# One decoder step with 32 routed experts: the second expert's first gate/up chunks moved ahead of the first one's down products, and the down bias moved into the first combine

## The chip, the cores and the metric
One of the eight cores of a Trainium2 chip runs the kernel, in float32 throughout. The metric is the device time of one execution in microseconds. Before the change it is 1125.2, the median of three runs (1124.46 to 1127.17).

## The reference
288 tokens (256 of a prompt, 8 x 4 of running sequences) of width 1024 go through one layer: windowed attention with sinks beside an S5 state-space branch, an output projection, and then the part that the change is about, a mixture of 32 experts with the top 4 for each token:

```python
logits = x2d @ w_router + b_router
top_v, top_i = lax.top_k(logits, 4)
gates = softmax(top_v)
# for the tokens of each expert e:
h = xb @ w_gate_up[e] + b_gate_up[e]                      # 1024 -> 2048
out = _clamped_swiglu(h) @ w_down[e] + b_down[e]          # 1024 -> 1024
y = segment_sum(out * row_w, row_tok)                     # gate-weighted sum per token
x = x + y
```

The weights of an expert are 8.4 MB (gate/up) and 4.2 MB (down), so all 32 are 403 MB.

## The kernel before, in words
**The layer ahead of the experts** takes the first 190 us and is not touched.

**The order of the experts.** On the device the experts are sorted by how many tokens they have. Experts 0 and 1 come first whatever their number. A place in the order has a fixed kind (KINDS, line 50): "mid" takes 64 slots of tokens, "few" 32, "many" 64 and 32. The first places are mid, mid, few, many, few, mid, few, many. Places 2 to 17 are a loop of four places with four rounds; later places follow in another loop. p is the place, w counts the wide (64-slot) passes so far and s the slim (32-slot) ones. Items that overflow their slots would run in a loop at the end, which has none to do with these inputs.

**The work of one place on TensorE** (expert, line 1052) is written out by hand:
- gate_up, eight chunks of 128 input rows. A wide pass has four matmul calls for a chunk, alternating between two 64-column halves of the array. Each call of float32 is two matmul records in the trace, so a chunk is 8 records. PSUM banks 0 and 1 collect gate and up (bank 5 for slim).
- Between chunks 1 and 2, the gate matrix of the place before is transposed (turn_gates, line 994). Between chunks 3 and 4, and again later, comes one half of combine (line 1008): it multiplies the expert output ye of the place before with the transposed gates gT, and VectorE adds the result to the residual xT (accumulate, line 1974). Half a combine of a wide pass has four calls, two on the upper and two on the lower 64 rows of the array.
- turn_hidden (line 916) transposes gate and up results, which ScalarE and VectorE copy out and turn into hT (hidden, line 1928).
- gather and turn_gathered (lines 855, 873) pick the tokens of the next place with a one-hot matmul into bank 5, and transpose them. ScalarE copies the result to xe, the input of the next gate_up.
- down (line 950): eight chunks of the down product into bank 4, which ScalarE copies to ye.

Place 0 has no place before it. There gate_bias (line 1037) stands in for combine: it adds the gate-weighted down bias of all experts, with bdnT (bias) and gT, four calls for a half, each on another 32 rows. Its four results go through accumulate as well, so that the semaphores comb_done and acc_done count 4 for each place.

**The weights** come through rings in SBUF: gu_ring has four slots of two chunks (2048 KB each), so one expert, and dn_ring four of half a down matrix, so two experts. SyncE's queue issues every load, in a fixed order (load_others, line 370). A load waits for gu_used (one count for each chunk) or dn_used (one for each quarter of a down product), so for TensorE to be done with what lies in the slot. Expert 0's gate/up and both first down matrices are loaded ahead. Expert 1's gate/up follows as eight pieces of 1024 KB, each as soon as the chunk of expert 0 in its place is used (lines 388 to 390). From then on it is, for each place, the down halves of the place two ahead and then the four gate/up slots of the next one but one.

Of the kernel before, what the change touches and what calls it, by code (L numbers as in the profile page):

```python
# [23 lines left out]
P = 128  # L24
# [53 lines left out]
def build(nc, a):  # L78
# [152 lines left out]
    pos_next = sb("pos_next", [3], o); o += 32  # L231
    assert o <= WK + 3456, (o, WK + 3456)
# [12 lines left out]
    bdnT = sb("bdnT", [2 * P], o); o += 1024  # L245
    grid = sb("grid", [ITEM_PART, REPEATS * NE], o); o += sz(ITEM_PART, REPEATS * NE)
# [123 lines left out]
    def load_others(sp):  # L370

        regs = [sp.alloc_register(f"sp_at{k}") for k in range(2)]

        def expert_at(k, p):
            sp.reg_load(regs[k], ord_e[0:1, p:p + 1] if isinstance(p, int) else ord_e[0:1, bass.ds(p, 1)])
            return sp.snap(regs[k], min_val=0, max_val=NE - 1)

        def gu(x, p_before):
            for k in range(GU_SLOTS):
# [73 lines left out]
    def _(sp):  # L453
# [70 lines left out]
        for k, c in enumerate((0, 2, 1, 3)):  # L524
            sp.wait_ge(S("acc_done"), items * 4 + (4 * NE + (4 if k else 2)))
# [7 lines left out]
    def _(pe):  # L533
# [353 lines left out]
        def gate_up(p, w, s, kind, chunks):  # L887
# [6 lines left out]
            for k in chunks:  # L894
# [3 lines left out]
                if kind != "few":  # L898
                    for part in range(2):
                        for h in range(2):  # L900
                            f = part * D + h * HALF
                            last = mm(pb[part][SLOTS * h:SLOTS * h + SLOTS, :], xe[:, k % 4, k // 4],
# [105 lines left out]
        def combine(p, w, s, kind, halves=(0, 1)):  # L1008

            if kind != "few" and halves[0] == 0:  # L1010
                pe.wait_ge(S("gT_ready"), w + 2)
                pe.wait_ge(S("ye_ready"), w + 1)
# [3 lines left out]
            for half in halves:  # L1016
                if half and kind != "mid":
                    pe.wait_ge(S("acc_done"), p * 4 + 2)
                if kind != "few":
                    for n in range(2):  # L1020
                        c = 2 * n + half
                        if half and kind == "mid":
                            pe.wait_ge(S("acc_done"), p * 4 + (n + 1))
# [13 lines left out]
        def gate_bias(halves):  # L1037

            pe.wait_ge(S("gT_ready"), 1)
            pe.wait_ge(S("bias_ready"), 2)  # L1040
            for i in halves:
                for n in range(2):
                    if i:
                        pe.wait_ge(S("acc_done"), n + 1)
                    for h in range(2):
                        q = 2 * h + n
                        rows = slice(NE * q, NE * q + NE)
                        last = mm(pb[(2, 6)[n] + h][:, 0:T], bdnT[rows, i * P:(i + 1) * P], gT[rows], True, True,
                                  tile_position=(NE * q, 0))
                    last.then_inc(S("comb_done"), 1)  # L1050

        def expert(p, w, s, kind, before, after, j, fill):
# [3 lines left out]
            gate_up(p, w, s, kind, range(0, 2))  # L1056
            if before == "bias":
                turn_gates(0)
            else:
                if before == "many":  # L1060
                    pe.wait_ge(S("ye_s_ready"), s_before + 1)
                if before != "few":
                    turn_gates(w)
                if before != "mid":
                    turn_gates_s(s_before)
            second = 7 if kind == "few" else 6
            gate_up(p, w, s, kind, range(2, 4))
            for half, rows in enumerate((range(4, second), range(second, 8))):
                if before == "bias":
                    gate_bias((half,))  # L1070
                else:
                    combine(p, w_before, s_before, before, (half,))
                gate_up(p, w, s, kind, rows)
            if kind != "few":
                pe.wait_ge(S("acc_done"), p * 4 + 3)
# [3 lines left out]
            pe.wait_ge(S("acc_done"), p * 4 + 4)  # L1079
# [18 lines left out]
        expert(0, 0, 0, KINDS[0], "bias", KINDS[1], 0, 1)  # L1098
        expert(1, 1, 0, KINDS[1], KINDS[0], KINDS[2], 1, 1)
# [16 lines left out]
        with pe.If_cmp(n, 0, "IS_GT"):  # L1116
            pe.wait_ge(S("acc_done"), 4 * (NE + 1))
# [3 lines left out]
            with pe.Fori(0, n) as j:  # L1121
                gate_up(j + NE, j + N_WIDE, N_SLIM, "mid", range(8))
                pe.wait_ge(S("acc_done"), j * 4 + 4 * (NE + 1))
# [10 lines left out]
    def _(act):  # L1134
# [234 lines left out]
        def act_turned(g):  # L1369

            act.wait_ge(S("xe_turned"), g + 1)
            A(xe[:].rearrange("p c h s -> p (c h s)"), pb[6][:], ACT.Copy).then_inc(S("xe_ready"), 1)

        def act_gates(b):

            act.wait_ge(S("g_turned"), b + 1)
            A(gT[:], pb[7][:, 0:T], ACT.Copy).then_inc(S("gT_ready"), 1)
# [44 lines left out]
        def act_expert(p, w, s, kind, before, after):  # L1422

            w_after, s_after = w + (kind != "few"), s + (kind != "mid")
            if before == "bias":
                act_gates(0)
            else:
                if before != "few":
                    act_gates(w)
                if before != "mid":  # L1430
                    act_gates_s(s - 1)
# [27 lines left out]
        act_expert(0, 0, 0, KINDS[0], "bias", KINDS[1])  # L1459
# [13 lines left out]
        for n in (1, 3):  # L1473
            act.wait_ge(S("comb_done"), 4 * NE + (n + 1))
# [19 lines left out]
    def _(dve):  # L1494
# [479 lines left out]
        def accumulate(b):  # L1974
            for n, c in enumerate((0, 2, 1, 3)):
                two = xT[:, c::4]
                dve.wait_ge(S("comb_done"), b * 4 + (n + 1))
# [65 lines left out]
        def expert(p, w, s, kind, before, after, x):  # L2043
# [3 lines left out]
            if before != "bias":  # L2047
                if before != "few":
                    gated(slots_of(x_before), bass.ds(x_before, 1), w)
                if before != "mid":  # L2050
                    gated_s(slots_of(x_before), SLOTS if before == "many" else 0, bass.ds(x_before, 1))
# [11 lines left out]
        expert(0, 0, 0, KINDS[0], "bias", KINDS[1], (0, 0, 1))  # L2063
# [32 lines left out]
        dve.wait_ge(S("comb_done"), 4 * NE + 1)  # L2096
        two, summed = last_pair(*LAST_PARTS[0][:2])
        X.tensor_tensor(two, two, summed, ALU.add).then_inc(S("acc_done"), 2)
        dve.wait_ge(S("comb_done"), 4 * NE + 3)
# [3 lines left out]
        with dve.If_cmp(n, 0, "IS_GT"):  # L2103
            dve.wait_ge(S("tail_done"), 2)
            with dve.Fori(0, n) as j:
# [4 lines left out]
                dve.wait_ge(S("acc_done"), j * 4 + 4 * (NE + 1))  # L2110
# [143 lines left out]
```

## Time and profile before

| | us |
|---|---|
| median of three runs | 1125.2 |
| lowest and highest | 1124.46, 1127.17 |
| the profiled execution, its own time | 1126.02 |
| its span, first to last instruction | 1123.8 |
| TensorE busy in it | 1000.4 (89%) |
| VectorE busy | 395.9 (35%) |
| ScalarE busy | 206.2 (18%) |
| mean granted TensorE clock | 0.963 |
| HBM read in it | 419.86 MB |

The span is what the rows of the trace lie in, and their times count from its start; 2.2 us of the execution lie around it. A busy TensorE is one with a matmul in flight; the ends of matmuls are modelled, so that the time that a group holds the engine is read from its start to the start of the next group.

### The profile page before, as it was taken

Reading aid. Unit: us, or ns where it says so; the run is one execution under the profiler, and the core shown is the slowest. Engines: PE = TensorE matmul, PEld = TensorE weight load, DVE = VectorE, ACT = ScalarE, POOL = GpSimd, SP = SyncE. Lnnn points to the kernel's source line nnn. Section 1 sums busy time; section 2 is a strip of 40 time slices with the busy share of each in tenths; the row PEclk is TensorE's granted clock in tenths of the full one; section 3 lists DMA queues with packets and bytes.
Section 4 is the critical chain, followed back from the end, with each engine's and each line's share of the span. In section 5 each row is a group of like instructions: output and inputs, shape, how many; then the busy total and the mean of one; then the engine's idle time right before and its main releaser. Section 6 shows DMA issues by size and latency. Waiting matters only on the chain.

```text
span 1123.8 us, 16580 instructions
## 1 busy us (share of the span) xinstructions
PE 1000.4 (89%) x6600; PEld 430.1 (38%) x6600; DVE 395.9 (35%) x896; ACT 206.2 (18%) x443; POOL 7.0 (1%) x7
## 2 busy tenths in 40 slices
PE   6988999999998999979997999789779878979967
PEld 5766875333333333322332233233223323323323
DVE  6977637322322232221332132223323333222222
ACT  4676433111111111110110011111111111101101
POOL 1000000000000000000000000000000000000000
PEclk9966999999999999989999999999989999989999
DMA  9513672999999999999999999999999999999996
GB/s 360 174 47 95 280 309 94 355 425 427 427 411 426 426 428 426 428 427 426 420 428 425 427 426 428 428 427 427 428 428 427 426 427 427 429 428 427 428 419 249
DMA packets 39292, 426.27 MB, mean 379 GB/s; under 512 B 7060, under 2 KB 10260, under 8 KB 12720
## 3 DMA queue, kind: packets, MB, share of 16 engines
q1 hardware_dynamic: 37440, 422.87, 90.0%
q10 hardware_dynamic: 1728, 2.11, 0.6%
q8 instruction: 63, 1.03, 0.4%
q0 software_dynamic: 48, 0.15, 0.0%
q14 instruction: 13, 0.11, 0.0%
HBM read 419.86 MB, written 2.51 MB: 376 GB/s over the span
## 4 chain that ended last, share of the span: by engine, by line
PE 60%; DMA 32%; DVE 3%; ACT 3%; issue 2%; ACTq 1%; DVEq 0%; SPq 0%
PE banks L535 57%; DMA gu_ring<-w_gu_dram 32%; PE banks L921 1%; DVE raw L1932 1%; PE banks L877 1%; PE banks L671 1%; ACT x_tok L1356 1%; ACT s_p L1268 1%; DVE hl L1944 0%; DVE hT L1949 0%; PE banks L928 0%; PE banks L998 0%; ACT gath L1367 0%; PE banks L1005 0%; ACT raw_s L1411 0%
## 5 line engine op out<-in xcount | busy, mean ns | idle before, releaser
L1978 DVE TENSOR_TENSOR xT<-xT,banks 128x576 f32<-128x576 f32 x128 | 91.1, 751 | 533.7 <-PE banks L535 533.7
L535 PE MATMUL banks<-gu_ring,xe 128*64 128x512 f32 x1152 | 266.3, 599 | 13.4 <-DMA gu_ring<-w_gu_dram 13.1
L535 PE MATMUL banks<-gu_ring,xe_s 128*32 128x512 f32 x1152 | 157.4, 646 | 43.3 <-DMA gu_ring<-w_gu_dram 33.6
L535 PEld LDWEIGHTS banks<-gu_ring,xe 128*64 128x64 f32 x1152 | 75.3, 136 | 166.6 <-issue 139.9
L535 PE MATMUL banks<-dn_ring,hT 128*64 128x512 f32 x576 | 129.3, 597 | 5.0 <-DVE hT L1949 5.0
L535 PEld LDWEIGHTS banks<-gu_ring,xe_s 128*32 128x32 f32 x1152 | 29.2, 112 | 133.6 <-issue 84.5
L535 PE MATMUL banks<-dn_ring,hT_s 128*32 128x256 f32 x1152 | 67.8, 381 | 3.3 <-ACT xe_s L1401 3.2
L535 PEld LDWEIGHTS banks<-dn_ring,hT 128*64 128x64 f32 x576 | 39.2, 137 | 79.4 <-issue 73.0
L1382 ACT ACTIVATE raw<-banks 128x512 f32<-128x512 f32 x18 | 10.7, 597 | 233.9 <-PE banks L535 233.9
L535 PE MATMUL banks<-x_tok,oh 96*64 96x512 f32 x216 | 50.3, 601 | 0.0
L535 PE MATMUL banks<-gT,ye 64*128 64x288 f32 x288 | 50.0, 471 | 0.0
L535 PEld LDWEIGHTS banks<-dn_ring,hT_s 128*32 128x32 f32 x1152 | 35.0, 110 | 36.2 <-issue 15.1
L535 PEld LDWEIGHTS banks<-gT,ye 64*128 64x128 f32 x288 | 27.8, 208 | 38.7 <-issue 34.1
L1411 ACT ACTIVATE raw_s<-banks 128x512 f32<-128x512 f32 x18 | 10.7, 597 | 169.0 <-PE banks L535 169.0
L535 PE MATMUL banks<-xg,w_in 128*128 128x288 f32 x160 | 39.8, 406 | 0.0
L1391 ACT ACTIVATE ye<-banks 128x512 f32<-128x512 f32 x18 | 10.7, 597 | 136.0 <-PE banks L535 136.0
L535 PEld LDWEIGHTS banks<-xg,w_in 128*128 128x128 f32 x160 | 30.4, 190 | 8.4
L535 PE MATMUL banks<-aT,w_out 128*128 128x288 f32 x128 | 32.3, 410 | 1.0 <-ACT aT L1307 1.0
L1932 DVE COPY raw<-banks 128x512 f32<-128x512 f32 x18 | 12.4, 692 | 55.6 <-PE banks L535 55.6
L921 PE MATMUL banks<-ident,raw 128*128 128x128 f32 x144 | 26.8, 309 | 2.2
L535 PE MATMUL banks<-gT_s,ye_s 32*128 32x288 f32 x288 | 27.4, 452 | 0.6 <-ACT ye_s L1420 0.6
L921 PEld LDWEIGHTS banks<-ident,raw 128*128 128x128 f32 x144 | 20.0, 207 | 20.3 <-issue 14.7
(352 smaller groups left out, 879.1 us busy)
## 6 DMA issues: line engine op xcount, KB each, us to landing
gu_ring<-w_gu_dram SPq DMA_DIRECT2D x120, 2048.0 KB, 24.2
dn_ring<-w_dn_dram SPq DMA_DIRECT2D x63, 2048.0 KB, 21.1
gu_ring<-w_gu_dram SPq DMA_DIRECT2D x16, 1024.0 KB, 8.7
w_out<-w_out_dram SPq DMA_DIRECT2D x2, 2048.0 KB, 10.1
w_in<-w_in_dram SPq DMA_DIRECT2D x3, 1024.0 KB, 16.2
w_in<-w_in_dram SPq DMA_DIRECT2D x4, 512.0 KB, 10.3
W<-W1c SPq DMA_DIRECT2D x16, 128.0 KB, 2.3
w_glu<-w_glu_dram SPq DMA_DIRECT2D x1, 2048.0 KB, 8.5
```

Of the source, the lines that this page charges most:

```text
L535: return nc.tensor.matmul(out, lhsT, rhs, start=start, stop=stop, **kw)
L671: last = pe.transpose(bank[0:m, i * P:(i + 1) * P], src, ident[:])
L877: last = pe.transpose(pb[6][:, c * P:(c + 1) * P], gath[:, c * P:(c + 1) * P], ident[:])
L921: last = pe.transpose(pb[2 + part][:, c * P:(c + 1) * P], hidden_cols(raw[:, part], c), ident[:])
L1268: last = A(ap, ap, ACT.Copy, scale=st_sum[:, i:i + 1])
L1356: A(half.rearrange("p (s i f) -> p s f i", i=GU_ROWS, f=P), pb[XB[u]][0:MT, :].rearrange("p (s f i) -> p s f i", i=GU_ROWS, f=P), ACT.Copy ...
L1382: A(blocks_out(raw[:, 0]), blocks_in(pb[0]), ACT.Copy).then_inc(S("g_copied"), 1)
L1391: A(ye[:], pb[4][:], ACT.Copy, scale=0.5).then_inc(S("ye_ready"), 1)
L1411: A(blocks_out(raw_s[:]), blocks_in(pb[5]), ACT.Copy).then_inc(S("raw_s_ready"), 1)
L1932: X.tensor_copy(blocks_out(raw[:, 1]), blocks_in(pb[1])).then_inc(S("l_copied"), 1)
L1978: X.tensor_tensor(two, two, pair[(1, 3)[n % 2]].rearrange("p (h f) -> p h f", h=2)[:, :, 0:T], ALU.add).then_inc(S("acc_done"), 1)
```

## The change
In TensorE's program, place 0 becomes first_expert: its gate/up chunks follow each other without gate_bias; the gather for expert 1 stands behind chunk 5 and its transposes behind chunk 6; and expert 1's first two gate/up chunks stand behind turn_hidden, ahead of expert 0's down products. Expert 1 then begins with its gate transposes. In its two halves of combine each matmul call is followed by one of the bias, into the same accumulation. Since the gather runs while expert 0's input is still in use, its result goes to a second tile, xe_next; the gates for the bias stay in gT_bias. SyncE's queue gets the two halves of expert 2's first gate/up slot as two loads, each waiting for its own chunk, ahead of expert 2's down loads. ScalarE's and VectorE's programs follow the new order. The other hunks lower the counts of comb_done and acc_done by 4, since gate_bias no longer counts.

```diff
+    xe_next = sb("xe_next", [4, 2, SLOTS], o); o += 2048
+    gT_bias = sb("gT_bias", [T], o)
...
-        return p * 16 + 16 * (2 * GU_ROWS - 1)
+        return p * 16 + 16 * (2 * GU_ROWS - 1 + (GU_ROWS - 1 if k == 0 else 0))
...
-        with sp.Fori(0, PAIRS - 2) as i:
-            x = [expert_at(k, i * 2 + (k + 2)) for k in range(2)]
-            dn(x[0], i * 2, 0)
-            gu(x[0], i * 2 + 1)
-            dn(x[1], i * 2 + 1, 1)
-            gu(x[1], i * 2 + 2)
+        x = [expert_at(k, 2 + k) for k in range(2)]
+        for r in range(GU_ROWS):
+            sp.wait_ge(S("gu_used"), 8 + r + 1)
+            half = a["w_gu"][bass.ds(x[0], 1), 0:GU_ROWS].rearrange("o k p f -> (o k p) f").rearrange(
+                "(p i) f -> p i f", i=GU_ROWS)[:, r]
+            sp.dma_start(gu_ring[0][:, r], half).then_inc(gu_in[0], 16)
+        dn(x[0], 0, 0)
+        gu(x[0], 1, range(1, GU_SLOTS))
+        dn(x[1], 1, 1)
+        gu(x[1], 2)
+        with sp.Fori(0, PAIRS - 3) as i:
+            x = [expert_at(k, i * 2 + (k + 4)) for k in range(2)]
+            dn(x[0], i * 2 + 2, 0)
...
@@ gate_up
+                            x = xe_next if isinstance(w, int) and w == 1 else xe
+                            last = mm(pb[part][SLOTS * h:SLOTS * h + SLOTS, :], x[:, k % 4, k // 4],
...
-        def combine(p, w, s, kind, halves=(0, 1)):
+        def combine(p, w, s, kind, halves=(0, 1), bias=False):
+            if bias:
+                pe.wait_ge(S("bias_ready"), 2)
...
                         for h in range(2):
                             rows = slice(SLOTS * h, SLOTS * h + SLOTS)
-                            last = mm(pb[(2, 6)[n] + h][:, 0:T], ye[rows, c * P:(c + 1) * P], gT[rows], True, kind == "mid")
+                            last = mm(pb[(2, 6)[n] + h][:, 0:T], ye[rows, c * P:(c + 1) * P], gT[rows], True,
+                                      kind == "mid" and not bias)
+                            if bias:
+                                q = 2 * h + n
+                                rows = slice(NE * q, NE * q + NE)
+                                last = mm(pb[(2, 6)[n] + h][:, 0:T], bdnT[rows, half * P:(half + 1) * P], gT_bias[rows],
+                                          False, True, tile_position=(NE * q, 0))
...
+        def first_expert():
+
+            gate_up(0, 0, 0, "mid", range(0, 2))
+            turn_gates(0)
+            gate_up(0, 0, 0, "mid", range(2, 6))
+            gather(1)
+            gate_up(0, 0, 0, "mid", range(6, 7))
+            turn_gathered(1)
+            gate_up(0, 0, 0, "mid", range(7, 8))
+            turn_hidden(0)
+            gate_up(1, 1, 0, "mid", range(0, 2))
+            down(0, 0, "mid", "mid", 0, 0, 1)
...
-        expert(0, 0, 0, KINDS[0], "bias", KINDS[1], 0, 1)
-        expert(1, 1, 0, KINDS[1], KINDS[0], KINDS[2], 1, 1)
+        first_expert()
+        expert(1, 1, 0, "mid", "mid", KINDS[2], 1, 1, begun=True)
...
@@ ScalarE
-        act_expert(0, 0, 0, KINDS[0], "bias", KINDS[1])
+        act_gates(0)
+        act_gathered(1)
+        act_turned(1)
+        act_gate(0)
+        act_tanh(0)
+        act_result(0)
...
@@ VectorE
-        expert(0, 0, 0, KINDS[0], "bias", KINDS[1], (0, 0, 1))
+        build_oh(slots_of(1), 1)
+        hidden(0, 0, 0, 0)
```

## Rows read from the trace of the kernel before

**Rows 1.** The page, span in 40 slices of 28.1 us: what the DMA moved
```profile
GB/s 360 174 47 95 280 309 94 355 425 427 427 411 426 426 428 426 428 427 426 420 428 425 427 426 428 428 427 427 428 428 427 426 427 427 429 428 427 428 419 249
```

**Rows 2.** Stretches: window, length, busy us of PE, PEld, DVE, ACT, POOL; PEclk, DMA share, GB/s
```profile
218.00:220.00 2.00, 2.00 (x12) 0.68 (x10) 0.00 (x0) 0.00 (x0) 0.00 (x0) 1.00 0.05 20
220.00:222.00 2.00, 2.00 (x12) 0.62 (x10) 0.00 (x0) 0.00 (x0) 0.00 (x0) 1.00 0.80 164
...
308.00:310.00 2.00, 2.00 (x24) 0.85 (x24) 0.00 (x0) 0.00 (x0) 0.00 (x0) 1.00 0.76 320
310.00:312.00 2.00, 2.00 (x30) 0.76 (x30) 0.00 (x0) 0.00 (x0) 0.00 (x0) 1.00 1.01 287
```

**Rows 3.** SyncE's queue in time: start, from first to last issue, line, load
```profile
219.41 3.76 SPq L344 DMA_DIRECT2D dn_ring<-w_dn_dram  x2
...
247.92 3.76 SPq L344 DMA_DIRECT2D dn_ring<-w_dn_dram  x2
...
309.24 4.06 SPq L344 DMA_DIRECT2D dn_ring<-w_dn_dram  x2
```

**Rows 4.** All waits of PE, 193 to 313 us: waiter, released by, total, times, longest
```profile
PE banks L884 <- ACT gath_s L1396: 1.1, 2, 0.6
PE banks L928 <- ACT raw_s L1411: 0.7, 1, 0.7
PE banks L877 <- ACT gath L1367: 0.7, 1, 0.7
PE banks L535 <- ACT xe_s L1401: 0.7, 1, 0.7
PE banks L535 <- DVE hT L1949: 0.7, 2, 0.5
PE banks L535 <- ACT xe L1372: 0.3, 1, 0.3
```

**Rows 5.** PE in time, experts 0 and 1: start, us, operands, records, idle before
```profile
193.81 3.65 PE L535 MATMUL banks<-gu_ring,xe 128*64 128x512 f32 x16 [0.25 <-ACT xe L1372]
...
197.79 3.65 PE L535 MATMUL banks<-gu_ring,xe 128*64 128x512 f32 x16
201.38 0.77 PE L535 MATMUL banks<-gT,bdnT 32*128 32x288 f32 x8
202.07 3.65 PE L535 MATMUL banks<-gu_ring,xe 128*64 128x512 f32 x16
...
209.94 1.61 PE L921 MATMUL banks<-ident,raw 128*128 128x128 f32 x8
211.48 2.80 PE L535 MATMUL banks<-x_tok,oh 96*64 96x512 f32 x12
214.97 0.66 PE L877 MATMUL banks<-ident,gath 128*128 128x128 f32 x4 [0.70 <-ACT gath L1367]
215.56 7.09 PE L535 MATMUL banks<-dn_ring,hT 128*64 128x512 f32 x32
...
226.01 0.47 PE L998 MATMUL banks<-ident,goh 96*128 96x96 f32 x3
```

**Rows 6.** DVE in time, the end of expert 0's hidden chain
```profile
213.78 0.69 DVE L1949 SCALAR_TENSOR_TENSOR hT<-th,hl 128x512 f32<-128x512 f32 x1
```

**Rows 7.** PE in time, half a combine behind a "many" place
```profile
316.92 1.24 PE L535 MATMUL banks<-gT,ye 64*128 64x288 f32 x8
318.09 0.77 PE L535 MATMUL banks<-gT_s,ye_s 32*128 32x288 f32 x8
```

**Rows 8.** PE in time, near the end: the residual's matmuls inside the last down products
```profile
1112.52 1.24 PE L535 MATMUL banks<-xT,ident 128*128 128x288 f32 x4
1113.69 1.93 PE L535 MATMUL banks<-dn_ring,hT_s 128*32 128x256 f32 x32
```

**Rows 9.** PE in time, attention values: one 32-row call between 128-row ones
```profile
111.74 0.43 PE L535 MATMUL banks<-pT,v_tok 32*64 32x128 f32 x2
112.09 1.96 PE L535 MATMUL banks<-pT,cacheV 128*64 128x128 f32 x16
```

More of the change, by code:

```diff
@@ L376, in expert_at, with gu @@
             return sp.snap(regs[k], min_val=0, max_val=NE - 1)
-        def gu(x, p_before):
-            for k in range(GU_SLOTS):
+        def gu(x, p_before, slots=range(GU_SLOTS)):
+            for k in slots:
                 sp.wait_ge(S("gu_used"), p_before * 8 + GU_ROWS * (k + 1))
@@ L391, in load_others @@
         sp.wait_ge(S("order_ready"), 1)
-        with sp.Fori(0, PAIRS - 2) as i:
-            x = [expert_at(k, i * 2 + (k + 2)) for k in range(2)]
-            dn(x[0], i * 2, 0)
-            gu(x[0], i * 2 + 1)
-            dn(x[1], i * 2 + 1, 1)
-            gu(x[1], i * 2 + 2)
+        x = [expert_at(k, 2 + k) for k in range(2)]
[11 more added lines that the diff above has]
+            dn(x[0], i * 2 + 2, 0)
+            gu(x[0], i * 2 + 3)
+            dn(x[1], i * 2 + 3, 1)
+            gu(x[1], i * 2 + 4)
         x = [expert_at(k, NE - 2 + k) for k in range(2)]
@@ L1035, in combine, with expert @@
                         last.then_inc(S("comb_done"), 1)
[L1037 to L1052, printed above, removed]
+        def first_expert():
[9 more added lines that the diff above has]
+            down(0, 0, "mid", "mid", 0, 0, 1)
+        def expert(p, w, s, kind, before, after, j, fill, begun=False):
             w_before, s_before = w - (before != "few"), s - (before != "mid")
             w_after, s_after = w + (kind != "few"), s + (kind != "mid")
[L1056 to L1065, printed above, removed]
+            if not begun:
+                gate_up(p, w, s, kind, range(0, 2))
+            if before == "many":
+                pe.wait_ge(S("ye_s_ready"), s_before + 1)
+            if before != "few":
+                turn_gates(w)
+            if before != "mid":
+                turn_gates_s(s_before)
             second = 7 if kind == "few" else 6
@@ L1068, in expert @@
             for half, rows in enumerate((range(4, second), range(second, 8))):
[L1069 to L1072, printed above, removed]
+                combine(p, w_before, s_before, before, (half,), begun)
                 gate_up(p, w, s, kind, rows)
             if kind != "few":
-                pe.wait_ge(S("acc_done"), p * 4 + 3)
+                pe.wait_ge(S("acc_done"), (p - 1) * 4 + 3)
                 turn_hidden(w)
@@ L1078, in expert @@
                 turn_hidden_s(s)
-            pe.wait_ge(S("acc_done"), p * 4 + 4)
+            pe.wait_ge(S("acc_done"), (p - 1) * 4 + 4)
             if after in ("mid", "many"):
@@ L1116, in _ @@
         with pe.If_cmp(n, 0, "IS_GT"):
-            pe.wait_ge(S("acc_done"), 4 * (NE + 1))
+            pe.wait_ge(S("acc_done"), 4 * NE)
             pe.wait_ge(S("tail_done"), 2)
@@ L1371, in act_turned @@
             act.wait_ge(S("xe_turned"), g + 1)
-            A(xe[:].rearrange("p c h s -> p (c h s)"), pb[6][:], ACT.Copy).then_inc(S("xe_ready"), 1)
+            dst = xe_next if isinstance(g, int) and g == 1 else xe
+            A(dst[:].rearrange("p c h s -> p (c h s)"), pb[6][:], ACT.Copy).then_inc(S("xe_ready"), 1)
         def act_gates(b):
             act.wait_ge(S("g_turned"), b + 1)
-            A(gT[:], pb[7][:, 0:T], ACT.Copy).then_inc(S("gT_ready"), 1)
+            dst = gT_bias if isinstance(b, int) and b == 0 else gT
+            A(dst[:], pb[7][:, 0:T], ACT.Copy).then_inc(S("gT_ready"), 1)
         def act_gate(e):
@@ L1424, in act_expert @@
             w_after, s_after = w + (kind != "few"), s + (kind != "mid")
[L1425 to L1431, printed above, removed]
+            if before != "few":
+                act_gates(w)
+            if before != "mid":
+                act_gates_s(s - 1)
             if kind != "few":
@@ L2046, in expert @@
             w_after, s_after = w + (kind != "few"), s + (kind != "mid")
[L2047 to L2051, printed above, removed]
+            if before != "few":
+                gated(slots_of(x_before), bass.ds(x_before, 1), w)
+            if before != "mid":
+                gated_s(slots_of(x_before), SLOTS if before == "many" else 0, bass.ds(x_before, 1))
             if after != "few":
```

19 lines of the change are left out of this document (9 added, 10 removed).

## The prediction
> **What bounds the kernel now.** The slices come first: from the ninth on, bar two a little below, the DMA moves 425 GB/s or more until the last weights arrive [rows 1]. From there to the end the kernel is one stream of expert weights, and its end moves only if the stream starts sooner or stands idle for more or less time. A block of 2048 KB takes 2.097 MB / 427 GB/s = 4.91 us; an expert is six of them.
>
> The second look is at the holes in that stream. At 218 to 222 us it is 407 and 263 GB/s short over 2 us each, at 308 to 312 it is 107 and 140 short [rows 2]: 3.1 us of idle in the first hole, 1.2 in the second. SyncE issues a load when PE has finished with the buffer. The first hole lies around the down load issued at 219.41, the second around the one issued at 309.24 [rows 3]: all loads that PE had made room for were done, and the stream waited for PE.
>
> The third look is at PE between the holes. From 193 to 313 us it waits for ACT and DVE in eight short waits, 4.2 us in all, and never for a weight load [rows 4]. So **up to the hole at 308 the kernel is bound by PE**, and how late PE is at expert 3's down products passes whole into the stream. A gain ahead of 308 counts only as far as PE comes to those products earlier.
>
> **The change on PE, part by part.** Before, from expert 0's first gate/up matmul (193.81) to the end of its down products and expert 1's first two chunks (226.01) it is 32.2 us [rows 5]. The new order, from the same rows:
> - Chunks 0 and 1 with the gate transposes: 3.98, unchanged.
> - Chunks 2 to 5, gather(1) and chunk 6: 32 + 12 + 8 = 52 records of one layout. The 48 from 215.56 to 226.01 took 10.45: 0.2135 each and 0.2 once. So 11.3.
> - turn_gathered: 0.59. Its wait for ACT's copy (0.70 before) now lies beside chunk 6, which takes 1.7; without that cover it would cost 0.7 again.
> - Chunk 7: 8 x 0.2135 + 0.17 = 1.88. turn_hidden: 1.54.
> - Expert 1's chunks 0 and 1, then down(0): again 48 records, 10.45. hT was ready 4.53 us after turn_hidden began (209.94 to 214.47) [rows 5, 6]; now 1.54 + 3.6 = 5.1 us of PE work stand ahead of down(0), so it is hidden, with 0.6 to spare.
>
> Sum: 3.98 + 11.3 + 0.59 + 1.88 + 1.54 + 10.45 = 29.7. **PE gains 2.5 us**: 1.4 from the two gate_bias groups, 0.7 from the gather's wait, the rest from fewer changes of layout. ACT keeps its order, with result(0) last; DVE loses four additions and is not on the path; POOL is not touched. SyncE issues expert 2's first slot as two halves ahead of dn(x[0]), one issue more on its queue. They wait for gu_used 9 and 10, which come at some 214.9 and 216.7; what is queued behind them, the down loads, waits for dn_used, which comes at 220, so none is held back. The halves put 2 MB, 4.9 us of work, into the first hole. xe_next and gT_bias only keep data apart, and renumbered semaphores cost nothing.
>
> **The bias in the first combine** is the dear part. Half a combine is four matmul calls (8 records) of 64 rows and holds PE for 1.17 us (316.92 to 318.09) [rows 7]. gate_bias, four calls of 32 rows, held it for 0.69 (201.38 to 202.07) [rows 5]. Four records of 128 rows also take 1.17 [rows 8]. So 64-row calls run two at a time and 32-row calls four at a time: 1.17 is 4 records in a row, 0.70 is 2. A record is then 0.235, and each group pays 0.23 for the change of layout. The new loop puts a 32-row bias call behind each 64-row call: y, b, y, b, y, b, y, b. Neighbours never have the same layout, and a group is one call, 2 records in a row. Upper bound of a group: 2 x 0.235 + 0.23 = 0.70. Lower bound: the one 32-row call that stands alone between others took 0.35 (111.74 to 112.09) with 128 columns [rows 9]; less 2 x 0.235 x 128/288 = 0.21 that leaves 0.14 for the change, so 0.61. I take 0.67, nearer to the upper, since its weights are 128 columns wide as here and the other's 64. Half a combine costs 8 x 0.67 = 5.4 in place of 1.17, and the two halves add 8.4 us (7.4 at the lower bound, 8.9 at the upper).
>
> The Trainium skill, TensorEngine Tiling (Array Packing), Key Properties, says that changing the tiling mode, and not just the tile, drains the engine. By that rule, each of the eight groups stands alone, at the sum taken here. The rows agree as far as they go, with the remainder of 0.14 to 0.23 at every change of layout; none shows 64-row and 32-row calls in turn.
>
> **Sum.** PE reaches expert 2 by 8.4 - 2.5 = 5.9 us later (4.9 to 6.4). In the stream the first hole is filled. But expert 2's third and fourth slots come free at some 236.4 and 245.4 and its loads run out at 242.4 and at 251.4, for about 4 and 3 us. So the down load of 247.92 [rows 3] starts about 4 us later than before, less late than PE, and PE still meets no missing weights up to expert 3. There the load of 309.24 is issued at 315.1 and the stream resumes 5.9 later. Nothing behind gives that back, as the stream runs full there. The profiled execution (1126.02, its span of 1123.8 and 2.2 around it) becomes 1131.9. It lay 0.8 above the median of the runs, 1125.2, so the median becomes **1131.1 us**.
>
> **The rivals.**
> 1. *Layouts overlap* (0.16). A bias call starts while a 64-row call streams in the other half of the rows. With the two halves of the rows as free queues half a combine is 8 x 0.235 + 0.23 = 2.1, adding 1.9 in all; with calls that must start in order it is 13 record times, 3.3, adding 4.3. Net -0.6 to +1.8: 1124.6 to 1127.0. For it: within one layout calls do overlap [rows 7]. Against it: the remainder of 0.23 also where 64-row calls give way to 32-row ones. The same page of the Trainium skill says that tiles operate independently. Were that to hold across modes, this rival would be the outcome.
> 2. *Faster* (0.06): the bias calls cost what they cost as a group, 0.70 a half. PE ends 2.5 - 1.4 = 1.1 us earlier, at 1124.1. The change breaks even where a group costs (2.5 + 2 x 1.17) / 16 = 0.30; below that it gains. Against it: one call's records alone take 0.47 in a row, so that needs calls of unlike layouts to overlap fully.
> 3. *The stream alone counts* (0.05). If loads queued ahead cover PE's delay, the filled hole moves the end by 3.1: 1122.1. For it: the full slices [rows 1]. Against it: the hole at 308, where nothing was queued.
> 4. *A further wait on PE* (0.03): if down(0) or turn_gathered waits after all, 0.7 each, and groups cost 0.75: 5.9 + 1.4 + 1.3, at 1133.8.
>
> **Chances.** Forecast 0.70; its own range 1129.5 to 1132.8 is 4.9 to 6.4 with 0.6 below and 1.2 above for the spread of the runs (1124.46 to 1127.17). The whole range also takes in most of rival 1: 1125.3 to 1132.8. A measurement here tells a change from none at about 0.3%, 3.4 us, so slower is above 1128.6: forecast and rival 4, 0.73. Same is rivals 1, 2 and most of 3: 0.25. Faster, below 1121.8: 0.02.
>
> **What would show it.** Expert 1's two halves of combine should hold PE for 5.4 us each (2 to 3.3 by rival 1, 1.9 by rival 2). Its first chunk should start near 213.1 and down(0) near 216.6, with no wait between. The stream at 218 to 220 should read above 400 GB/s in place of 20 [rows 2], with idle near 242 to 246 and 251 to 254. The load of 309.24 should be issued near 315. The forecast is wrong if the combine stays short, or if that load is late and the end is not.

## The result, and the profile after

The kernel after takes 1135.05 us (median of six runs, 1134.62 to 1137.85); the kernel before, run beside it, 1124.83 (six runs, 1122.97 to 1127.23). The ratio is 1.0089, with an interval of 1.0075 to 1.0103: 10.0 us more, between 8.4 and 11.6. The change makes the kernel slower, as forecast, but by 10 us where 5.9 were predicted and the range ended at 7.6.

The page of the kernel after; its own time is 1135.2 us and its span 1133.4:

```profile
PE 1011.3 (89%) x6600; PEld 430.7 (38%) x6600; DVE 393.2 (35%) x892; ACT 206.3 (18%) x443; POOL 7.0 (1%) x7
...
PEclk9978999989999999999998999999989989999989
...
GB/s 357 173 47 100 344 310 59 415 279 379 430 391 429 424 428 426 428 424 430 425 427 427 427 409 428 428 426 428 427 425 430 426 427 428 427 428 427 427 421 254
```

Against [rows 1] the stream starts better in the eighth slice (415 for 355), then falls to 279 and 379 in the ninth and tenth, from 227 to 283 us, where it ran full before. Behind the twelfth slice the two rows are alike. So the loss lies in one place, and what PE does there comes next. These are PE's instructions from expert 0's first chunk to expert 2's first chunk: start, us, line, operands, records, idle before in brackets.

```profile
191.98 3.65 PE L547 MATMUL banks<-gu_ring,xe 128*64 128x512 f32 x16 [0.25 <-ACT xe L1387]
...
211.26 3.65 PE L547 MATMUL banks<-gu_ring,xe_next 128*64 128x512 f32 x16
214.75 7.04 PE L547 MATMUL banks<-dn_ring,hT 128*64 128x512 f32 x32
221.72 0.47 PE L1011 MATMUL banks<-ident,goh 96*128 96x96 f32 x3
...
225.70 0.75 PE L547 MATMUL banks<-gT,ye 64*128 64x288 f32 x2
226.38 0.75 PE L547 MATMUL banks<-gT_bias,bdnT 32*128 32x288 f32 x2
...
230.12 1.32 PE L547 MATMUL banks<-gT,ye 64*128 64x288 f32 x2
231.38 1.32 PE L547 MATMUL banks<-gT_bias,bdnT 32*128 32x288 f32 x2
232.63 5.39 PE L547 MATMUL banks<-gu_ring,xe_next 128*64 128x512 f32 x16
237.96 0.75 PE L547 MATMUL banks<-gT,ye 64*128 64x288 f32 x2
...
243.70 4.98 PE L547 MATMUL banks<-gu_ring,xe_next 128*64 128x512 f32 x16
248.62 1.60 PE L934 MATMUL banks<-ident,raw 128*128 128x128 f32 x8
...
260.21 1.92 PE L547 MATMUL banks<-gu_ring,xe_s 128*32 128x512 f32 x16
```

Three things are to be seen. The moves gave what was asked of them: from the first chunk to expert 1's gate transposes it is 221.72 - 191.98 = 29.74 us, where [rows 5] have 32.20, and no wait stands in it. A group of two records alone between others lasts 226.38 - 225.70 = 0.68, as priced at 0.67. But later in the same half the same group lasts 1.26 (230.12 to 231.38), and the two chunks behind a half, one kind of row with 16 records, take 5.33 (232.63 to 237.96) and 4.92 where the first row of the fence takes 3.6. All of these are the same instructions at two speeds. The stretches say why. Columns as in [rows 2]: window, length, busy us of PE, PEld, DVE, ACT, POOL; PEclk, DMA share, GB/s.

```profile
218.00:220.00 2.00, 2.00 (x12) 0.67 (x10) 0.00 (x0) 0.00 (x0) 0.00 (x0) 1.00 1.00 418
...
225.00:229.00 4.00, 4.00 (x14) 1.47 (x10) 0.48 (x1) 0.00 (x0) 0.00 (x0) 1.00 0.99 422
229.00:230.00 1.00, 1.00 (x3) 0.29 (x2) 0.27 (x1) 0.00 (x0) 0.00 (x0) 0.67 1.04 442
230.00:236.00 6.00, 6.00 (x13) 2.00 (x14) 0.75 (x1) 0.00 (x0) 0.00 (x0) 0.50 0.95 404
...
237.00:243.00 6.00, 6.00 (x21) 2.49 (x18) 0.75 (x1) 0.00 (x0) 0.00 (x0) 1.00 0.63 216
243.00:246.00 3.00, 3.00 (x8) 0.77 (x8) 0.75 (x1) 0.00 (x0) 0.00 (x0) 0.50 0.63 268
246.00:250.00 4.00, 3.88 (x20) 1.69 (x16) 1.27 (x2) 0.60 (x1) 0.00 (x0) 0.95 0.15 33
```

**The granted clock fell to 0.50**, the lower of its two levels (1.2 for 2.4 GHz), between 229 and 230 us in the first half and near 243 in the second, and stayed there into the chunks behind each, until a little past 236 and 246. PE shows as busy for 100% of the windows up to 246; what it did before each fall was nothing but groups of two records on 64 and on 32 rows in turn. That column is no proof that nothing stood still inside a group: two records in a row take 2 x 0.235 = 0.47 (an estimate from [rows 5] and [rows 7]), and a group holds PE for 0.68. The other falls behind 193 us, nine in the trace of before and ten in this one, look different: shortly before each of them PE had been idle, busy for 3% at most of a whole microsecond. One of them, at 372 us:

```profile
368.00:372.00 4.00, 2.46 (x12) 0.57 (x8) 0.00 (x0) 0.60 (x1) 0.00 (x0) 1.00 1.05 442
372.00:376.00 4.00, 3.11 (x16) 0.61 (x16) 0.00 (x0) 0.00 (x0) 0.00 (x0) 0.59 0.95 406
```

The Trainium skill, TensorE: Matmul & The Clock Gate, Part 1, ties the clock to how busy TensorE has lately been and gives idle time as what lowers it; at these nineteen that is what the rows show, but at 229 and 243 us no row shows any idle, so its rule fits there only if "busy" is something else than the busy column.

The first line also shows that the first hole is filled, 418 GB/s in place of 20, as predicted, and the last that the stream is dry again soon after: 33 GB/s at 246 to 250, for slots that PE has not freed yet.

The waits of PE, 192 to 325 us, stand where [rows 4] had eight: the gather's wait for gath (0.7) is gone, the others are the same ones; of the list, PE's waits in its products:

```profile
...
PE banks L547 <- ACT xe_s L1417: 0.7, 1, 0.7
PE banks L547 <- DVE hT L1967: 0.7, 2, 0.5
PE banks L547 <- ACT xe L1387: 0.3, 1, 0.3
```

SyncE's queue (start, from first to last issue, line, load) has the two loads of [rows 3] here:

```profile
257.02 3.77 SPq L346 DMA_DIRECT2D dn_ring<-w_dn_dram  x2
...
318.36 4.06 SPq L346 DMA_DIRECT2D dn_ring<-w_dn_dram  x2
```

Two quantities make the kernels comparable, since expert 0 starts anywhere from 190.9 to 193.9 us in executions of one and the same kernel. **PE's delay** is the time from expert 0's first chunk to expert 2's first chunk: before 57.29, after 68.23, so +10.94. Counted in the same way, the load of 309.24 is issued at 115.43 before and at 126.38 after, +10.95: PE's delay, whole. **The idle time of the stream** is the sum over stretches of (427.3 - GB/s) / 427.3 x length. In us, by the stretch counted from expert 0's first chunk (the last one in steps of 20 us):

| profiled execution of | 20 to 32 | 32 to 110 | 110 to 170 | 170 to 850 | sum | own time less expert 0's start |
|---|---|---|---|---|---|---|
| before | 3.2 | 0.1 | 1.2 | 0.8 | 5.1 | 932.2 |
| before, second one (e0_before) | 3.0 | 0.1 | 1.4 | 1.7 | 6.2 | 933.0 |
| after | 0.0 | 12.8 | 2.3 | 1.6 | 16.7 | 943.2 |
| e1_grouped | 0.0 | 1.0 | 2.4 | 1.0 | 4.3 | 930.2 |
| e3_y128 | 0.0 | 8.1 | 2.3 | 0.9 | 11.3 | 937.2 |
| e10_onehalf | -0.1 | 7.7 | 2.4 | 0.9 | 10.9 | 937.2 |
| e4_nobias | -0.1 | 0.1 | 2.0 | 0.5 | 2.5 | 928.8 |
| e6_oldqueue | 4.1 | -0.1 | 0.2 | 2.2 | 6.3 | 932.2 |
| e7_manylater | -0.1 | 1.0 | 0.0 | 8.1 | 9.0 | 935.6 |
| e9_latebias | 0.0 | 0.1 | 1.7 | 0.7 | 2.5 | 929.2 |

The kernel after is 10.5 to 11.6 above the two of before, and its time 10.0. The kernel is one stream, and its idle time is its loss: the last two columns move together, to within about 1 us of the mean of the two of before.

### The profile page after: what moved, and what is told of

Read it like the earlier page. It is cut to its first block, busy times and chain, and to the rows that moved or that the text cites. A ratio compares the mean times of both kernels' runs of the same rounds, so it can differ in the third digit from the quotient of the medians.

```text
span 1133.4 us, 16590 instructions
## 1 busy us (share of the span) xinstructions
PE 1011.3 (89%) x6600; PEld 430.7 (38%) x6600; DVE 393.2 (35%) x892; ACT 206.3 (18%) x443; POOL 7.0 (1%) x7
## 4 chain that ended last, share of the span: by engine, by line
PE 60%; DMA 30%; DVE 4%; ACT 3%; issue 2%; ACTq 1%; DVEq 0%; SPq 0%
PE banks L547 57%; DMA gu_ring<-w_gu_dram 30%; PE banks L934 1%; DVE raw L1950 1%; PE banks L889 1%; ACT x_tok L1370 1%; ACT s_p L1282 0%; PE banks L941 0%; DVE hT L1967 0%; DVE hl L1962 0%; PE banks L683 0%; PE banks L1011 0%; ACT raw_s L1427 0%; PE banks L1018 0%; ACT gath L1381 0%
## 5 line engine op out<-in xcount | busy, mean ns | idle before, releaser
L1996 DVE TENSOR_TENSOR xT<-xT,banks 128x576 f32<-128x576 f32 x124 | 88.5, 751 | 533.7 <-PE banks L547 533.7
L547 PE MATMUL banks<-gu_ring,xe 128*64 128x512 f32 x1088 | 253.4, 603 | 12.2 <-DMA gu_ring<-w_gu_dram 11.9
L547 PEld LDWEIGHTS banks<-gu_ring,xe 128*64 128x64 f32 x1088 | 71.4, 137 | 157.8 <-issue 131.9
L547 PE MATMUL banks<-gT,ye 64*128 64x288 f32 x288 | 53.6, 470 | 0.8 <-issue 0.8
```

Source lines behind the costliest of these rows:

```text
L547: return nc.tensor.matmul(out, lhsT, rhs, start=start, stop=stop, **kw)
L1996: X.tensor_tensor(two, two, pair[(1, 3)[n % 2]].rearrange("p (h f) -> p h f", h=2)[:, :, 0:T], ALU.add).then_inc(S("acc_done"), 1)
```

## The experiments

A call's layout is here the number of rows of the array that it covers (128, 64 or 32). Theory: the calls of the bias, 32 rows between neighbours of 64, isolate each group (5.4 us a half in place of 1.17), and the run of such groups lets the granted clock fall, which costs the rest. Rival A: the calls of the bias cost what they do whatever the order, since they are more work. Rival B: the clock falls for what the moves do to PE or to the DMA. Rival C: the new order of the loads, not PE, makes the dry spells.

| run | median us | ratio to before, 95% | PE's delay against before |
|---|---|---|---|
| after | 1135.05 | 1.0089 (1.0075 to 1.0103) | +10.94 |
| e0_before | 1123.95, one run | | 0.00 |
| e1_grouped | 1122.6 | 0.998 (0.997 to 0.999) | -1.07 |
| e2_bias64 | 1123.99 | 0.999 (0.998 to 0.9999) | -0.32 |
| e3_y128 | 1129.34 | 1.003 (1.0018 to 1.0042) | +6.08 |
| e4_nobias | 1122.39 | 0.9966 (0.9954 to 0.9978) | -2.46 |
| e5_pairs | 1124.73 | 0.9998 (0.9987 to 1.001) | +0.68 |
| e6_oldqueue | 1124.44 | 0.9998 (0.9987 to 1.0008) | -1.06 |
| e7_manylater | 1124.41 | 0.9989 (0.9976 to 1.0002) | -1.07 |
| e9_latebias | 1122.94 | 0.9977 (0.9967 to 0.9987) | -2.47 |
| e10_onehalf | 1129.08 | 1.0038 (1.0023 to 1.0052) | +5.75 |

### The same kernel again (e0_before)
The kernel before, unchanged.

> The kernel before, unchanged, for a second profile of it: the first profile began expert 0 at 193.81 us, those of the changed kernel and most of its variants near 192. Theory (the part ahead of the experts varies from one execution to the next by some 2 us, whatever the kernel): it begins anywhere from 191.6 to 194, and the time from there to expert 2's first chunk is 57.3 us again.

```profile
190.92 3.65 PE L535 MATMUL banks<-gu_ring,xe 128*64 128x512 f32 x16 [0.25 <-ACT xe L1372]
...
248.21 1.93 PE L535 MATMUL banks<-gu_ring,xe_s 128*32 128x512 f32 x16
```

PE, start and duration. From the first row to the second it is 57.29 us, in this execution as in the one of before, though both start 2.9 us earlier. PE's delay is therefore good to a few hundredths up to here. It is not further on: the idle time behind 170 us is 0.8 in one and 1.7 in the other. So differences of about 1 us between sums of idle time say nothing.

### The calls grouped by layout (e1_grouped)
```diff
-                            if bias:
-                                q = 2 * h + n
...
+                    for n in range(2 if bias else 0):
+                        for h in range(2):
+                            q = 2 * h + n
+                            rows = slice(NE * q, NE * q + NE)
+                            last = mm(pb[(2, 6)[n] + h][:, 0:T], bdnT[rows, half * P:(half + 1) * P], gT_bias[rows],
+                                      False, True, tile_position=(NE * q, 0))
+                        last.then_inc(S("comb_done"), 1)
```
The same calls in the order y, y, y, y, b, b, b, b.

> The changed kernel, with the bias calls of a half of combine placed behind all four 64-row calls of it (y y y y b b b b). Theory (unlike layouts cannot overlap, each single call costs 0.68 us, and the single calls also let the TensorE clock fall): half a combine takes 1.17 + 0.70 = 1.87 us, the clock stays at full speed from 225 to 250 us, TensorE reaches expert 2's first chunk 1.1 us earlier than in the kernel before (counted from expert 0's first chunk), and the time is 1.1 us below the kernel before, some 1123.7. Rival (the moved chunks or the extra load cost time themselves, and the bias order does not matter): the time stays more than 3 us above the kernel before.

PE in time, the first half of combine of expert 1:

```profile
225.38 1.24 PE L547 MATMUL banks<-gT,ye 64*128 64x288 f32 x8
226.55 0.77 PE L547 MATMUL banks<-gT_bias,bdnT 32*128 32x288 f32 x8
227.25 3.65 PE L547 MATMUL banks<-gu_ring,xe_next 128*64 128x512 f32 x16
```

A half takes 1.87 us (225.38 to 227.25) in place of 6.93, with the same records, and the chunks behind are at 3.65 again. PE's delay comes to -2.46 + 2 x 1.87 - 2.34 = -1.06, and -1.07 is measured; the kernel becomes 0.2% faster than before. Rivals A and B fall: all of the loss is in the order of the eight calls of each half. So does C in the main, since the new order of the loads is in this run too, and its dry spell behind 32 us is 1.0 where the kernel after has 12.8.

### Bias calls of the same layout, in the old order (e2_bias64)
```diff
                             if bias:
-                                q = 2 * h + n
-                                rows = slice(NE * q, NE * q + NE)
                                 last = mm(pb[(2, 6)[n] + h][:, 0:T], bdnT[rows, half * P:(half + 1) * P], gT_bias[rows],
-                                          False, True, tile_position=(NE * q, 0))
+                                          False, True)
```
Each bias call covers the 64 rows of its neighbour; it also sums the neighbouring block of 32 rows, so the bias that it adds is another one.

> The changed kernel, with its alternating order kept, but each bias call over 64 rows in place of 32, so that all eight calls of a half have one layout (the bias is then summed over the wrong rows: each call also takes in the neighbouring block of the bias). Theory (the change of layout is what isolates each call): 16 records two at a time, a half takes 8 x 0.235 + 0.23 = 2.1 us, the clock stays full, and the time is 2.5 - 1.9 = 0.6 us below the kernel before. Rival (two calls in a row into the same bank, or on the same rows, isolate them): a half stays at 5.4 us or more, the clock falls, and the time stays near 1135.

PE in time:

```profile
225.92 0.76 PE L547 MATMUL banks<-gT,ye 64*128 64x288 f32 x4
226.50 0.66 PE L547 MATMUL banks<-gT_bias,bdnT 64*128 64x288 f32 x4
...
228.16 3.65 PE L547 MATMUL banks<-gu_ring,xe_next 128*64 128x512 f32 x16
```

The half takes 2.24 us (225.92 to 228.16): calls of y and of the bias still alternate, twice as many records as in [rows 7] take about twice their 1.17, and nothing stands between them. Changing the tensor does not isolate a group; changing the rows does. The Trainium skill, TensorEngine Tiling (Array Packing), Key Properties, has this as a drain at a change of mode and none at a change of tile; this run and the kernel after agree with both halves of it.

### Half the groups on all rows (e3_y128)
```diff
-                            rows = slice(SLOTS * h, SLOTS * h + SLOTS)
+                            rows = slice(0, P) if bias else slice(SLOTS * h, SLOTS * h + SLOTS)
```
Each ye call multiplies all 128 rows, so each sum also takes in the products of the other 64 rows.

> The changed kernel, with its alternating order kept, but each call of ye over all 128 rows in place of 64 (it then sums both halves of the output, which is not the reference's). The calls stay isolated by their layouts, with as many records of the same length, but half of them use the whole array. Theory A (the clock fell for how little of the array the single calls used): the groups stay at 0.68 us, a half at 5.4, the clock stays full or falls for less time, and the time is 5.9 us above the kernel before, near 1131. Theory B (the clock fell for the gaps between the groups, whatever part of the array works): the clock falls as in the changed kernel and the time stays near 1135.

PE in time, and the stretch that holds both halves:

```profile
225.75 0.75 PE L547 MATMUL banks<-gT,ye 128*128 128x288 f32 x2
226.44 0.75 PE L547 MATMUL banks<-gT_bias,bdnT 32*128 32x288 f32 x2
...
231.19 3.65 PE L547 MATMUL banks<-gu_ring,xe_next 128*64 128x512 f32 x16
```
```profile
225.00:241.00 16.00, 16.00 (x56) 6.12 (x54) 2.94 (x4) 0.00 (x0) 0.00 (x0) 1.00 0.98 397
```

This is the run that parts the two costs. The groups stay isolated, 0.69 each (225.75 to 226.44) and 5.44 a half, which is the 5.4 of the prediction, but the clock holds at 1.00 throughout and the chunks behind take their 3.65. PE's delay is +6.08, against 5.9 predicted. So on PE the isolation alone does what was forecast, and the 4.9 us that the kernel after loses there beyond it (10.94 - 6.08) come with the clock. The groups take as long as in the kernel after at full clock, so whatever stands still inside a group stands still here too, and yet the clock holds. The half of the rows that lay unused in the 64-row calls is what differs; how the chip reckons it no run here shows.

The time did not follow PE in full: 5.9 us more than before was expected, and 0.3% is measured, 3.4 us, between 2.0 and 4.7. Up to 170 us behind expert 0's start the stream has lost what PE has (8.1 + 2.3 against 3.2 + 0.1 + 1.2 in before, 5.9 more), so the difference arises behind that; no run shows where.

### Without the bias (e4_nobias)
```diff
-                combine(p, w_before, s_before, before, (half,), begun)
+                combine(p, w_before, s_before, before, (half,))
```
Leaves the down bias out of the whole computation.

> The changed kernel without the bias calls in expert 1's combine (the down bias of all experts is left out of the result). Theory: a half takes 1.17 us, the clock stays full, TensorE reaches expert 2 some 2.5 us earlier than before, and since the stream waits for TensorE at the down load of expert 3, the time is 2.5 us below the kernel before, 1122.3. Rival (the stream alone counts, and its first hole is filled): 3.1 to 3.3 us below, and as much in the grouped version. Rival (the moved parts cost time themselves): not below the kernel before.

PE's delay is -2.46, the gain of the moves alone: place 2's first chunk stands at 248.77 where expert 0 began at 193.94, so 54.83 for 57.29. The kernel gains 0.34% (0.22 to 0.46), some 3.8 us (2.5 to 5.2), which is if anything more than PE's 2.46; the idle time sums to 2.5, against 5.1 and 6.2. It bounds what the change could have brought with the bias free.

### In pairs (e5_pairs)
```diff
-                            if bias:
-                                q = 2 * h + n
...
+                        for h in range(2 if bias else 0):
+                            q = 2 * h + n
...
```
The order y, y, b, b, y, y, b, b.

> The changed kernel, with two 64-row calls and then the two bias calls of the same output pair (y y b b y y b b). Theory (a change of layout isolates, calls of one layout pair up): four groups of 0.70 us, a half takes 2.8 us, the clock stays full, TensorE is 2.46 - 2 x 1.63 = 0.8 us later at expert 2 than before, and the time is 0.8 us above the kernel before. If the clock falls at such groups too, a half is longer than 2.8 us and the rows show a granted clock of 0.5 there.

PE in time, and the stretch with both halves:

```profile
227.41 0.76 PE L547 MATMUL banks<-gT,ye 64*128 64x288 f32 x4
228.09 0.76 PE L547 MATMUL banks<-gT_bias,bdnT 32*128 32x288 f32 x4
...
230.15 3.65 PE L547 MATMUL banks<-gu_ring,xe_next 128*64 128x512 f32 x16
```
```profile
227.00:240.00 13.00, 13.00 (x68) 4.52 (x64) 3.01 (x4) 0.60 (x1) 0.00 (x0) 1.00 1.01 430
```

A group of two calls side by side takes 0.68, as much as one call alone: four groups make 2.74 for a half where eight made 5.4. This is the plainest sign that the price goes by the change of layout and not by the call. The clock stays at 1.00 here too. The calls are those of the kernel after, but two of them run side by side, and a half is over after 2.74 us; which of the two holds the clock up this run does not tell. The kernel is level with the one before.

### One alternating half (e10_onehalf)
```diff
-                            if bias:
+                            if bias and half == 0:
...
+                    for n in range(2 if bias and half else 0):
...
```
The first half of combine as in the kernel after, the second grouped as in e1_grouped.

> The changed kernel with the alternating order in the first half of the combine only, and the grouped order in the second. Theory (both the isolated calls and the fall of the clock that follows them cost): the first half takes 6.9 us and the two chunks behind it 5.3, the granted clock there is 0.5, as in the changed kernel; the second half takes 1.87 and its chunks 3.58 at full clock; TensorE is 10.95 - (5.74 - 1.87) - (4.92 - 3.58) = 5.7 us late at expert 2, and the time is 5.7 us above the kernel before. Rival (the clock falls only after both halves, or by chance): 2.5 us late without a fall.

PE in time, and the stretch at the end of the first half:

```profile
229.83 1.33 PE L547 MATMUL banks<-gT,ye 64*128 64x288 f32 x2
...
232.34 5.50 PE L547 MATMUL banks<-gu_ring,xe_next 128*64 128x512 f32 x16
237.77 1.24 PE L547 MATMUL banks<-gT,ye 64*128 64x288 f32 x8
238.94 0.77 PE L547 MATMUL banks<-gT_bias,bdnT 32*128 32x288 f32 x8
239.64 3.65 PE L547 MATMUL banks<-gu_ring,xe_next 128*64 128x512 f32 x16
```
```profile
230.00:236.00 6.00, 6.00 (x14) 2.02 (x16) 0.76 (x1) 0.00 (x0) 0.00 (x0) 0.50 0.93 396
```

One alternating half is enough for a fall, at the same place as in the kernel after, and the grouped half brings none: 1.87 for it (237.77 to 239.64), 3.65 for the chunks. PE's delay is +5.75, where 5.7 was expected. The time is 0.38% more than before (0.23 to 0.52), 4.3 us for the 5.7 expected, with 5.8 at the end of its interval.

### Grouped, with the loads in their old order (e6_oldqueue)
```diff
...
-        for r in range(GU_ROWS):
-            sp.wait_ge(S("gu_used"), 8 + r + 1)
...
-        dn(x[0], 0, 0)
-        gu(x[0], 1, range(1, GU_SLOTS))
...
+        with sp.Fori(0, PAIRS - 2) as i:
+            x = [expert_at(k, i * 2 + (k + 2)) for k in range(2)]
+            dn(x[0], i * 2, 0)
+            gu(x[0], i * 2 + 1)
...
```
On top of e1_grouped.

> The grouped version (y y y y b b b b) with the queue of loads as in the kernel before: expert 2's first gate/up slot is one load, issued behind the down loads, so that the first hole in the stream, near 220 us, comes back. Theory (the stream waits for TensorE again at expert 3's down products, so what the first hole gives is lost there): the hole at 218 to 222 us is 1 to 3 us again, the one near 306 gets smaller by as much, TensorE's course is that of the grouped version, and the time is within 0.5 us of it, near 1122.6. Rival (the filled hole moves the end): 2 to 3 us above the grouped version.

The two holes, in e6_oldqueue, and the second in e1_grouped (columns as before):

```profile
218.00:220.00 2.00, 2.00 (x12) 0.65 (x10) 0.00 (x0) 0.00 (x0) 0.00 (x0) 1.00 0.59 123
...
304.00:308.00 4.00, 4.00 (x37) 1.19 (x37) 0.00 (x0) 0.00 (x0) 0.00 (x0) 1.00 1.00 422
```
```profile
304.00:308.00 4.00, 4.00 (x36) 1.19 (x36) 0.00 (x0) 0.00 (x0) 0.00 (x0) 1.00 0.67 213
```

With the old order the stream stands idle for 4.1 us in the first hole and hardly at all in the second; with the new one it is 0.0 and 2.4, with 1.0 between. PE is at the same point in both (-1.06 and -1.07). So filling the first hole mostly moves the idle time to the next place at which the stream waits for PE: 4.2 becomes 3.4. The sums of idle time are 2.0 apart, but 1.2 of that lies behind 170 us, where two executions of one kernel differ by 0.9. Measured, e6_oldqueue was 1.8 slower, where at most 0.5 had been expected; the ratios of the two differ by 0.0018, and their intervals overlap. Rival C falls as far as harm goes: the new order costs nothing. What it is worth this does not settle: 0.8 us of idle time up to 170 us behind expert 0's start, 1.8 by the medians.

### The larger place later (e7_manylater)
```diff
-BODY, ROUNDS = ("few", "many", "few", "mid"), 4
+BODY, ROUNDS = ("few", "few", "many", "mid"), 4
```
On top of e1_grouped, to close the hole at 308, which lies behind the first "many" place.

> The grouped version with the kinds of the loop's four places changed from few, many, few, mid to few, few, many, mid, so that the first 'many' expert, which holds TensorE for some 39 us, comes one place later and TensorE is ahead of the stream by then. Nothing else changes, and the same number of each kind is run. Theory (only the hole near 306 stands between the filled first hole and the end): the hole near 306 and the small one near 545 are gone, and the time is 2 to 3 us below the grouped version, near 1120. Rival (the stream is at its end anyway): no change against the grouped version. Rival (two slim experts in a row or the step from many to mid cost time on TensorE): above it.

What the DMA moved, in 40 slices:

```profile
GB/s 359 174 45 101 329 310 44 407 411 430 427 427 427 424 427 428 412 409 426 427 384 409 427 426 415 417 429 427 427 427 427 426 429 428 427 427 428 426 427 251
```

The hole at 308 is gone, but slices of 412 and 409, 384 and 409, 415 and 417 stand further on: with "many" and "mid" side by side PE falls behind the stream in several rounds, and the idle time behind 170 us is 8.1 where e1_grouped has 1.0. This execution took 1129.25, the longest of the twelve (1120.13 to 1129.25), so that how much of it is in the others is not shown. The expectation, 2 to 3 us below e1_grouped, was missed; the median, 1124.41, is no better than that of e1_grouped.

### The bias at the last place but one (e9_latebias)
```diff
-    gT_bias = sb("gT_bias", [T], o)
+    gT_bias = sb("gT_bias", [T], WK + 13824)
...
-        expert(NE - 2, N_WIDE, N_SLIM - 2, "few", "mid", "few", 0, PAIRS)
+        expert(NE - 2, N_WIDE, N_SLIM - 2, "few", "mid", "few", 0, PAIRS, bias=True)
```
On top of e1_grouped: the grouped bias calls stand at place 30, where PE waits for weights anyway, and gT_bias in memory that stays free until then.

> The grouped version with the bias moved once more, from expert 1's combine to that of place 30, where TensorE waits some 15 us for weights (gT_bias lies in memory that stays free until then). Theory (up to expert 3's down products every microsecond of TensorE counts, at place 30 none does): TensorE's course up to expert 3 is that of the version without bias, 2.46 us ahead of the kernel before, and the time is 2.5 us or a little more below the kernel before, as that of the version without bias (2.6 below), and 0 to 1.4 below the grouped one. Rival (in the grouped version the stream already sets the end): the same as the grouped version, 2.4 us below the kernel before at the latest comparison.

PE near its end, in e9_latebias:

```profile
1079.78 1.06 PE L547 MATMUL banks<-gu_ring,xe_s 128*32 128x512 f32 x8 [2.96 <-DMA gu_ring<-w_gu_dram]
1080.77 1.24 PE L547 MATMUL banks<-gT,ye 64*128 64x288 f32 x8
1081.94 0.77 PE L547 MATMUL banks<-gT_bias,bdnT 32*128 32x288 f32 x8
```

The same 0.70 for the bias of a half (1081.94 to 1082.64, where the next chunk starts) now stands behind a wait of 2.96 us for weights. PE's delay becomes -2.47, the whole gain of the moves, and the time 0.23% less than before (0.13 to 0.33). Both this version and e1_grouped beat both kernels; between the two (0.9977 and 0.998) no difference is measured. PE is 1.4 us earlier than in e1_grouped and the idle time 1.8 less (2.5 for 4.3), which the medians don't bear out; that stays open.

## Why the prediction was wrong

**What bounds the kernel** held up to that load: PE's delay passed whole into the stream (+10.94 at expert 2, +10.95 at the load of 309.24). That nothing behind gives it back held less well. The kernel after is 10.0 slower (8.4 to 11.6), which allows it; but e3_y128, which is the prediction's case with the clock at 1.00, is 3.4 slower (2.0 to 4.7) where PE's delay is 6.08. Had the clock held, then, the predicted 5.9 would have been too much, by an amount that stays open.

**The moves** held: 2.46 us gained, 2.5 predicted, with the chunks of expert 1 at 211.26 and down(0) at 214.75, each 1.8 before the places named, as this execution starts expert 0 1.83 earlier, and no wait between.

**The price of a group** held: 0.68 measured, 0.67 predicted, in the kernel after as long as the clock is at 1.00, and in e3_y128 for both halves. Rival 1, overlapping layouts, is out; so is rival 2, whose break-even of 0.30 a group is far off. Rivals 3 and 4 did not come about either: the stream alone did not count (e6_oldqueue, without the filled hole, is 1.8 slower than e1_grouped by the medians, not 3.1), and no wait was added.

**The step that failed** is "Half a combine costs 8 x 0.67 = 5.4 in place of 1.17", together with the chunks behind it, which were costed at nothing: all durations were taken at a granted clock of 1.00. The halves took 6.93 (225.70 to 232.63) and 5.74 (237.96 to 243.70), and the chunk pairs behind them 5.33 and 4.92 in place of 3.58. That is

-2.46 + (6.93 + 5.74 - 2 x 1.17) + (5.33 + 4.92 - 2 x 3.58) = -2.46 + 10.33 + 3.09 = 10.96,

for 10.94 measured, where the prediction had -2.5 + 8.4 = 5.9. The part that was missing, 1.9 in the halves and 3.1 behind them, is that of the clock. Of the orders tried, it comes only with 64- and 32-row calls one at a time in turn (not in e3_y128 nor in e5_pairs), and once for each half that has them (e10_onehalf). No row of before showed such calls, so the prediction bounded a group by its duration at full clock alone, and the range had no case in which the clock fell.

**The stream** went in kind as predicted, and further in size: the first hole filled (418 GB/s for above 400), then dry spells for 12.8 us in all where 7 were named, since the slots came free that much later. The down load of 309.24 was issued at 318.36, 115.43 + 10.95 us into the experts, where 315.1 was predicted.

## What to carry to other kernels

Before a matmul is put between others for nothing, look at which rows of the array each call uses: here a change of layout cost some 0.2 us each time, and it keeps neighbours from running side by side, so that four calls in a row took 0.70 us and one alone 0.68. Group calls by layout; the same sixteen calls cost 12.7 us in turn, the fall of the clock included, and 3.7 with two groups in each half. When small calls follow each other singly, ask what the granted clock will do and look at the PEclk column of their stretch, since full busy time does not vouch for it. And where a stream of loads waits for an engine at several places, filling the first gap is worth only what the next one does not take back.

## What the runs showed of the hardware that was not expected

The granted clock falls to 0.50 with TensorE busy for 100% of the time, when all it runs is single 64-row and 32-row calls in turn (at 229 to 230 us and again at 243), where every other fall behind 193 us in the traces of before and after has PE idle shortly ahead of it (busy for 3% at most of a microsecond); with 128-row calls in place of the 64-row ones (1.00 through 225 to 241), or with pairs of calls, which also finish a half sooner (1.00 through 227 to 240), it does not. It stayed down into the chunks behind, which use all 128 rows.

PE's course through the first two experts repeats between executions to a few hundredths of a us (57.29 and 57.29; e1_grouped -1.07, e6_oldqueue -1.06, e7_manylater -1.07), though its start varies by 3 us. A question about a few tenths of a us there is answered by one look at the trace, where the medians of many runs leave it open.
